# Output projection with four weight operands split once, products in another order over four banks, and the last head's tail in the next block

## The reference, cut to what matters

```python
h = rmsnorm(x, norm1_w); p = h @ w_in                    # x: 2048 x 1024, float32
qa, ka, va, qb, fb, ib, gb = split(p)
ya = window_attention(qa, ka, va)                        # 8 query heads, 2 kv heads, chunks of 64
# group B, 4 heads of 128, chunkwise:
fg = lb + (1 - lb) * sigmoid(fb); kh = 1 - fg; b = cumsum(log(fg)) within a chunk
att = (qh * exp(b - ref)) @ (kh * exp(ref - b)).T, causal
state[n + 1] = exp(b_last) * state[n] + (kh * exp(b_last - b)).T @ vh
yb = rmsnorm(att @ vh + (qh * exp(b)) @ state, g_norm_w) * silu(gb)
x = x + concat(ya, yb) @ w_out
h = rmsnorm(x, norm2_w); x = x + (silu(h @ w_gate) * (h @ w_up)) @ w_down
```

## Time and profile before

| what | value |
|---|---|
| median of three runs | 2230.67 us |
| the profiled execution's own time | 2232.16 us |
| its span, first to last instruction | 2230.4 us |
| PE busy | 2127.2 us (95%), 11512 matmuls |
| DVE busy | 1385.3 us (62%) |
| ACT busy | 908.1 us (41%) |
| mean granted clock of TensorE | 0.981 |
| blocks, and pairs of the projection | 18.1 to 760.6 us, 760.6 to 933 us |
| 1 MB load of an hx, issue to landing | 5.1 us |

### The profile page before, as it was taken

One profiled execution on the slowest core, in us unless ns is written; L12 is line 12 of the kernel. 1 busy time (PEld: TensorE's weight loads), 2 busy tenths in 40 slices (PEclk: granted clock), 3 DMA queues, 4 the chain that ended last, 5 costly groups with the idle time before them and its releaser, 6 DMA issues.

```text
span 2230.4 us, 29485 instructions
## 1 busy us (share of the span) xinstructions
PE 2127.2 (95%) x11512; PEld 1810.7 (81%) x11512; DVE 1385.3 (62%) x2030; ACT 908.1 (41%) x1526; POOL 102.8 (5%) x109
## 2 busy tenths in 40 slices
...
GB/s 264 143 76 57 95 110 67 78 113 76 67 119 90 154 179 244 212 153 131 149 158 151 151 99 168 188 174 170 147 179 137 171 260 179 198 173 187 180 137 90
DMA packets 173979, 327.67 MB, mean 147 GB/s; under 512 B 10321, under 2 KB 105809, under 8 KB 159377
## 3 DMA queue, kind: packets, MB, share of 16 engines
...
## 4 chain that ended last, share of the span: by engine, by line
PE 57%; DMA 0%; issue 0%; DVE 0%; POOLq 0%
PE b_bank_B L328 4%; PE b_bank_A L328 4%; PE b_bank_C L328 4%; PE b_bank_A L329 4%; PE b_bank_C L329 4%; PE b_bank_B L329 4%; PE b_bank_B L330 4%; PE b_bank_A L330 4%; PE b_bank_C L330 4%; PE b_hx_bank L1875 3%; PE b_hx_bank L1874 3%; PE b_hx_bank L1873 3%; PE b_bank_D L328 2%; PE b_bank_D L329 2%; PE b_bank_D L330 2%; PE b_hx_bank L1818 1%
## 5 line engine op out<-in xcount | busy, mean ns | idle before, releaser
L328 PE MATMUL a_pj<-a_w_hi,a_hT_hi 128*128 128x256 f32 x896 | 264.4, 295 | 1.5 <-DVE a_hT_lo L1160 1.5
L329 PE MATMUL a_pj<-a_w_lo,a_hT_hi 128*128 128x256 f32 x896 | 256.9, 287 | 0.0
L330 PE MATMUL a_pj<-a_w_hi,a_hT_lo 128*128 128x256 f32 x896 | 256.9, 287 | 0.0
L1761 ACT ACTIVATE b_s_hi<-b_s_stage 128x1408 fp32r<-128x1408 f32 x56 | 77.4, 1382 | 300.4 <-PE b_hx_bank L1875 150.1
L328 PEld LDWEIGHTS a_pj<-a_w_hi,a_hT_hi 128*128 128x128 f32 x896 | 175.4, 196 | 7.7 <-issue 2.7
L329 PEld LDWEIGHTS a_pj<-a_w_lo,a_hT_hi 128*128 128x128 f32 x896 | 175.5, 196 | 0.0
L330 PEld LDWEIGHTS a_pj<-a_w_hi,a_hT_lo 128*128 128x128 f32 x896 | 175.3, 196 | 0.0
L1146 DVE TENSOR_TENSOR a_w_lo<-a_w_stage,a_w_hi 128x2048 fp32r<-128x2048 f32 (+1 forms) x48 | 101.4, 2112 | 72.1 <-ACT a_w_hi L779 72.1
L328 PE MATMUL b_bank_B<-b_h_hi_T,b_w_hi 128*128 128x512 f32 x352 | 137.3, 390 | 0.0
L328 PE MATMUL b_bank_A<-b_h_hi_B,b_w_hi 128*128 128x512 f32 x352 | 137.3, 390 | 0.0
L330 PE MATMUL b_bank_A<-b_h_hi_B,b_w_lo 128*128 128x512 f32 x352 | 137.0, 389 | 0.0
...
## 6 DMA issues: line engine op xcount, KB each, us to landing
...
```

The lines of the kernel that those rows point to most:

```text
L328: pe.matmul(out, stationary[0](k), moving[0](k), start=(k == 0 and not adds), stop=False, skip_group_check=adds)
L329: pe.matmul(out, stationary[0](k), moving[1](k), start=False, stop=False, skip_group_check=adds)
L330: last = pe.matmul(out, stationary[1](k), moving[0](k), start=False, stop=(k == ends), skip_group_check=adds)
L1761: act.activation(f.s_hi[n % 2][:], f.s_stage[n % 2][:], ACT.Copy).then_inc(f.s_hi_ready, 1)
```

## The change

1. In every block `kt 0` and `ds 0` stand one group earlier. Head 3's `hb` and `hc` stand two groups and one group earlier, ahead of x's scaling; the x transposes 3 to 7 stand behind the last group; head 2's norm and head 3's `ds`, `att`, `o` and norm go behind the next block's first groups.
2. B21, T1, B11 and T2 (the first four operands used) are split once, in blocks 0 to 2: high and low parts are stored to DRAM, and block 3 loads both parts ready-made. Only B22, T4 and T3 are still split in pair 0. The four sets of `w_out` rows are worked on in block 0 (two), block 1 and block 2 (one each) instead of all in block 0.
3. The seven products stand in another order, the bank of each is written down, and a pair has four banks; even pairs use `pj` and `sc`, odd pairs `tr` and `[pvb, hb]`.
4. The squares and the store of a pair's first row come after five of its eight sums.
5. The second `hx` is loaded by SP at the end of the first stage too, and the head of the second stage is ordered anew.

```diff
-    after("G01", 2, ("pt", 4), ("pt", 5), ("sc", 3), ("att", 0), ("sm1", 6), ("sm1", 7), ("hb", 1))
-    after("G01", 3, ("kt", 0), ("sm2", 6), ("sm2", 7), ("pv", 2), ("hc", 1))
-    after("F23", 0, ("ds", 0, 0), ("ds", 0, 1), ("pt", 6), ("pt", 7))
+    after("G01", 2, ("pt", 4), ("pt", 5), ("sc", 3), ("att", 0), ("kt", 0), ("sm1", 6), ("sm1", 7), ("hb", 1))
+    after("G01", 3, ("ds", 0, 0), ("ds", 0, 1), ("sm2", 6), ("sm2", 7), ("pv", 2), ("hc", 1))
+    after("F23", 0, ("pt", 6), ("pt", 7))
...
-    after("I23", 1, ("on2", 1), ("on3", 1), ("split_lo", CHUNK_AT["G23"]), ("kt", 2), ("n1a",))
-    after("I23", 2, ("yt", 1), ("att", 2), ("n1b", 0), ("n1b", 1))
-    after("I23", 3, ("hb", 3), ("n1b", 2), ("n1b", 3))
-    after("G23", 0, ("xT", 0), ("ds", 2, 0), ("ds", 2, 1), ("hc", 3))
-    after("G23", 1, ("xT", 1), ("xT", 2), ("kt", 3))
-    after("G23", 2, ("o", 2), ("on1", 2), ("xT", 3), ("ds", 3, 0), ("ds", 3, 1))
-    after("G23", 3, ("xT", 4), ("xT", 5), ("xT", 6), ("xT", 7), ("on2", 2), ("on3", 2))
+    after("I23", 1, ("on2", 1), ("on3", 1), ("n1a",), ("kt", 2), ("hb", 3), ("split_lo", CHUNK_AT["G23"]))
+    after("I23", 2, ("yt", 1), ("att", 2), ("hc", 3))
+    after("I23", 3, ("n1b", 0), ("n1b", 1), ("n1b", 2), ("n1b", 3))
+    after("G23", 0, ("ds", 2, 0), ("ds", 2, 1))
+    after("G23", 1, ("xT", 0))
+    after("G23", 2, ("o", 2), ("on1", 2), ("kt", 3), ("xT", 1), ("xT", 2))
+    after("G23", 3, ("xT", 3), ("xT", 4), ("xT", 5), ("xT", 6), ("xT", 7))
...
-LAST_HEAD = {("KV", 0): (("att", HG - 1), ("yt", HG - 2)), ("KV", 1): (("o", HG - 1), ("on1", HG - 1)),
-             ("KV", 3): (("on2", HG - 1), ("on3", HG - 1)), ("QA0", 0): (("yt", HG - 1),)}
-PRODUCTS_OUT = ("P1", "P5", "P6", "P3", "P7", "P2", "P4")
+LAST_HEAD = {("KV", 0): (("on2", 2), ("on3", 2), ("ds", 3, 0), ("ds", 3, 1)), ("KV", 1): (("yt", 2), ("att", 3)),
+             ("KV", 2): (("o", 3), ("on1", 3)), ("KV", 3): (("on2", 3), ("on3", 3)), ("QA0", 1): (("yt", 3),)}
+PRODUCTS_OUT = ("P1", "P5", "P2", "P6", "P3", "P4", "P7")
+BANK_OUT = (0, 1, 2, 0, 1, 3, 0)
+READ_OUT = {"P6": 1, "P3": 2, "P7": 4}
+ROW_OUT = (5, 7)
...
+SPLIT_OUT = 4
+WO_BLOCK = (0, 0, 1, 2)
+def out_weight_sums(b):
+    if b == 0:
+        return {("KV", 0): (("wo_load", 0), ("wo_load", 1)), ("KV", 1): (("wo_sums", 0), ("wo_hi", 0)), ("KV", 2): (("wo_lo", 0),),
+                ("KV", 3): (("wo_store", 0), ("wo_sums", 1), ("wo_hi", 1)), ("QA0", 0): (("wo_lo", 1),), ("QA0", 1): (("wo_store", 1),)}
+    k = WO_BLOCK.index(b)
+    return {("KV", 0): (("wo_load", k),), ("KV", 3): (("wo_sums", k), ("wo_hi", k)), ("QA0", 0): (("wo_lo", k),), ("QA0", 1): (("wo_store", k),)}
...
 def out_prepared():
-            ("G23", 3): (("t_load", 4), ("t_load", 5), ("t_load", 6), ("t_hi", 3), ("a_hi", 0, 4), ("a_lo", 0, 2))}
+            ("G23", 3): (("on2", 2), ("on3", 2), ("a_lo", 0, 3), ("ds", 3, 0), ("ds", 3, 1), ("t_load", 4), ("t_load", 5), ("t_load", 6), ("a_hi", 0, 6))}
...
 def out_steps():
-    after(0, 0, ("t_lo", 3), ("a_hi", 0, 5), ("a_hi", 0, 6))
-    after(0, 1, ("t_hi", 4), ("a_load", 1))
-    after(0, 2, ("t_lo", 4), ("t_hi", 5), ("n2w_load",))
-    after(0, 3, ("t_lo", 5), ("t_hi", 6))
-    after(0, 4, ("t_lo", 6))
+    after(0, 0, ("yt", 2), ("att", 3), ("a_lo", 0, 4))
+    after(0, 1, ("o", 3), ("on1", 3), ("t_hi", 4), ("t_lo", 4), ("a_load", 1))
+    after(0, 2, ("t_hi", 5), ("t_lo", 5), ("on2", 3), ("on3", 3), ("a_lo", 0, 5), ("n2w_load",))
+    after(0, 3, ("t_hi", 6), ("t_lo", 6), ("a_lo", 0, 6))
+    after(0, 4, ("yt", 3),)
...
-            after(p, 5, ("a_sum", p + 1, "S4"), ("a_hi", p + 1, 2), ("a_hi", p + 1, 3), ("x_load", p + 1, 0), ("x_load", p + 1, 1), ("a_lo", p + 1, 0))
-            after(p, 6, ("a_hi", p + 1, 4), ("a_lo", p + 1, 1))
+            after(p, 5, ("a_hi", p + 1, 2), ("a_hi", p + 1, 3), ("x_load", p + 1, 0), ("x_load", p + 1, 1), ("a_lo", p + 1, 0), ("a_sum", p + 1, "S4"))
+            after(p, 6, ("a_hi", p + 1, 4), ("a_lo", p + 1, 1), ("a_lo", p + 1, 2))
...
-    out_banks = [pj, sc]
+    out_banks = [pj + sc, tr + [pvb, hb]]
...
+                elif kind == "wo_hi":
+                    k, s = step[1], wo_set(step[1])
+                    act.wait_ge(wo_ready, k + 1)
+                    if k >= 2:
+                        act.wait_ge(o_full.sem, o_full.upto(b - 1, HG))
+                    act.activation(wo_hi[s][:, 0:2, :], wo_blocks[s][:, 2:4, :], ACT.Copy)
+                    act.activation(wo_hi[s][:, 2:4, :], wo_sums[s][:], ACT.Copy).then_inc(wo_hi_ready, 1)
...
                 sp.dma_start(kept.hx[:], hc[0, HC.index(RIGHT[0])]).then_inc(kept.first_hx_loaded, 16)
+                sp.dma_start(kept.second_hx[:], hc[0, HC.index(RIGHT[1])]).then_inc(kept.second_hx_loaded, 16)
...
-        mix_weights(0)
-        w1_low(0)
+        dve.wait_ge(f.gu_loaded[0], 16)
+        w1_low_plain(0)
+        mix_weights(0)
         h_low(0, 0)
+        w1_low_mixed(0)
+        h_low(0, 1)
         w2_low(0)
-        h_low(0, 1)
```

More of the change, by code:

```diff
@@ L152, in of_next_block @@
     return step[0] in ("sq", "n1a", "n1b", "xT") or step[0] in ("split_hi", "split_lo") and step[1] == NW
-def out_weight_sums():
-    return {("KV", 0): (("wo_load", 0), ("wo_load", 1)), ("KV", 1): (("wo_sums", 0),), ("KV", 2): (("wo_store", 0),),
-            ("KV", 3): (("wo_sums", 1),), ("QA0", 0): (("wo_store", 1), ("wo_load", 2)), ("QA0", 2): (("wo_sums", 2), ("wo_load", 3)),
-            ("QA0", 3): (("wo_store", 2),), ("QA1", 0): (("wo_sums", 3),), ("QA1", 1): (("wo_store", 3),)}
-def out_prepared():
-    return {("KV", 0): (("t_load", 0),), ("KV", 2): (("t_hi", 0),), ("QA0", 0): (("t_lo", 0),),
-            ("Q01", 1): (("t_load", 1),), ("F23", 1): (("t_load", 2),), ("Q23", 1): (("t_hi", 1), ("x_load", 0, 0), ("x_load", 0, 1)),
-            ("I23", 0): (("t_lo", 1), ("a_load", 0)), ("I23", 1): (("t_hi", 2),), ("I23", 3): (("t_lo", 2),),
-            ("G23", 0): (("t_load", 3), ("a_sum", 0, "S1"), ("a_sum", 0, "S3")),
-            ("G23", 1): (("a_hi", 0, 0), ("a_hi", 0, 1), ("a_sum", 0, "S2"), ("a_sum", 0, "S4")),
-            ("G23", 2): (("a_hi", 0, 2), ("a_hi", 0, 3), ("a_lo", 0, 0), ("a_lo", 0, 1)),
-            ("G23", 3): (("t_load", 4), ("t_load", 5), ("t_load", 6), ("t_hi", 3), ("a_hi", 0, 4), ("a_lo", 0, 2))}
@@ new lines, in out_prepared @@
+def out_prepared():
+    return {("KV", 0): (("t_load", 0),), ("Q01", 1): (("t_load", 1),), ("F23", 1): (("t_load", 2),),
+            ("Q23", 1): (("x_load", 0, 0), ("x_load", 0, 1), ("a_load", 0)),
+            ("I23", 3): (("a_sum", 0, "S1"), ("a_sum", 0, "S3")),
+            ("G23", 0): (("t_load", 3), ("a_sum", 0, "S2"), ("a_sum", 0, "S4"), ("a_hi", 0, 0), ("a_hi", 0, 1)),
+            ("G23", 1): (("a_lo", 0, 0), ("a_hi", 0, 2), ("a_hi", 0, 3)),
+            ("G23", 2): (("a_lo", 0, 1), ("a_lo", 0, 2), ("a_hi", 0, 4), ("a_hi", 0, 5)),
+            ("G23", 3): (("on2", 2), ("on3", 2), ("a_lo", 0, 3), ("ds", 3, 0), ("ds", 3, 1), ("t_load", 4), ("t_load", 5), ("t_load", 6), ("a_hi", 0, 6))}
@@ L210, in out_steps @@
             after(p + 2, 1, ("mix", p, 3), ("mix_store", p))
-        after(p, 6, ("mid", p))
+        after(p, 5, ("mid", p, 0))
+        after(p, 6, ("mid", p, 1))
     after(OUT_PAIRS - 1, 0, ("next_loads",))
@@ L435, in build_phase_a @@
     wo_sums = [put(f"a_wo_sums{s}", [P, 2, 512], F32, at=at) for s, at in enumerate((spare_lo, f_at + 8192))]
+    wo_hi = [put(f"a_wo_hi{s}", [P, SPLIT_OUT, 512], F32R, at=at) for s, at in enumerate((i_at + 8192, i_at))]
     half = KT // 2 * TB * 4
@@ L454, in build_phase_a @@
     n2w = put("o_n2w", [P, D], F32, at=y_at)
+    kept.second_hx = put("b_hx1", [P, 4, 512], F32, at=y_at)
+    kept.second_hx_at = y_at
     mix_t = put("o_mix_t", [P, 3, 512], F32, at=y_at + D * 4)
```

205 lines of the change are left out of this document (116 added, 89 removed).

## The result

The kernel after takes 2159.56 us, median of 4 runs (2158.44 to 2159.83), beside 2231.24 us for the kernel before in the same comparison (2227.15 to 2232.1): a ratio of 0.9681, 95% interval 0.9665 to 0.9698, so 3.2% or about 71.7 us less. Forecast were 2154 us and a range of 2140 to 2180. One of the four executions of the run with part 1 undone took 3023.82 us at a granted clock of 0.654, in a slow state; it is left out of that run's median.

A forecast was written before the change was run, and what follows sets the result against it. The prediction took the kernel to be bound by PE's own program, busy 2127.2 of 2230.4 us. Terms 38.4 + 27.6 + 1.6 - 1.0 + 7.1 + 1.0 + 5.1 = 79.8, less 2.8, gave gain 77: 2154 us, range 2140 to 2180.

The forecast's parts named there:

- part 1: att 0 to pv 3, every block: kt 0 and ds 0 one group earlier; 9.6 us a block, 38.4 in all.
- late next: What PE waits for after the change; behind the state chain the softmax, pt 6 0.9 us and pt 7 0.6.
- Rival (a): Softmax and copies replace the chain as PE's wait, so less is gained in blocks: 2182 us, chance 0.17.
- Part 2: Blocks 0 to 2, from att 2: head 3's gates earlier, its ds, att, o in the next block; 27.6 us.
- 37.3 - 26.6 - 1.2 = 9.5: Block 1, att 2 to att 3: length less PE's work less small stands; 9.2 us taken as gain.
- Part 3: Weight operands split in blocks 0 to 2: front gains 1.6 us, blocks 1 and 2 lose 1.0.
- rival (d): F0's copy in blocks 1 and 2 waits for its stores, 10 us a block: 2174 us, chance 0.03.
- Part 4: Block 3's end and pair 0: no gates wait, three operands split; pair 1 begins 7.1 us earlier.
- Part 5: Pairs: product order, four banks, split mid; DVE's sum stays near 20.9 us, gain 1 us in all.
- rival (c): Pauses between products in four banks keep PE at 1.2 GHz in the pairs: 2252 to 2311 us, chance 0.02.
- Part 6: Hand-over to the second stage: second hx load's wait goes, DVE is late next; first product 5.1 us sooner.
- The charge for the lower clock: Deduction of 2.8 us because remaining stands in each F23 and pair 0 can bring the lower clock.

The follow-up runs named there:

- part 1 undone: Kernel after with kt 0 and ds 0 back at their old places in all four blocks: 2199.64 us, ratio 0.9863.
- the two experiments: kt 0 and ds 0 put back in the kernel after (40.1 us above it), and moved alone in the kernel before (39.4 us less than it).
- part 1 alone: Kernel before with only kt 0 and ds 0 one group earlier: 2192.06 us, ratio 0.9829.
- the run with late splits: Kernel after with all seven weight operands loaded raw and split in block 3 and pair 0, sums made in block 0 alone: 2158.75 us, ratio 0.968.
- the two-bank run: Kernel after with two banks for each pair's products, their order kept, output not the reference's: 2159.44 us, ratio 0.9683.
- the order run: Kernel after with the second stage's head reordered, hx 0's low part ahead of the plain low part and two mixing operations: 2156.96 us, ratio 0.9674.

## Why the prediction was right, and where its terms were off

**What bounds it, and part 1: right in mechanism and size.** 38.4 forecast, 38.8 read from the trace, 39.4 and 40.1 by the two experiments. The hand-followed order held to 0.1 us for the chain, and the stands that were named as "late next" are the ones seen: kt 0 1.03 us (1.1 forecast), pt 6 0.58 (0.9), pt 7 0.44 (0.6). Rival (a), the softmax in the chain's place, would have needed stands of 5 us; with the softmax put first, the cost was 2.9 us in all.

**Part 2: right in mechanism, too large by some 3 us.** 22.8 us plus the 1.8 us that the weight sets take in two of these stretches are 24.6, against 27.6. The step "37.3 - 26.6 - 1.2 = 9.5" held as far as it went: it puts KV's second group 27.8 us behind att 2, and 28.3 was measured. What failed is the list of small stands: it ends there and puts the next one at nothing. Head 2's `yt` was taken as work that follows freely; it waits for the end of head 3's state chain, which reads the state products of ds 3 on DVE, and ds 3 had just been moved to the group before. Moving `yt` behind att 3 gave 0.9 us a block, 2.7 of the 3.0 missing.

**Part 3: the loss in blocks 1 and 2 larger, the front's gain not shown.** Blocks 1 and 2 lost 1.8 us (0.9 each) instead of 1.0. The copy's delay was read correctly (0.5 forecast, 0.66 seen); the remaining 0.25 us of each 0.9 is not accounted for by a stand. The front won 0.9 us instead of 1.6. In stands it lost 0.3: 2.85 and 0.21 us for low parts of weights went, 1.40 and 1.96 came. What it won is the lower clock behind the 2.85 us, and that differs from one execution to the next (0.91 in the kernel before, 1.00 behind 2.77 us with part 1 alone). The last store was issued at 47.1 us and not near 41, and F0's copy still doesn't wait for it: in block 0 it waits for PE. ACT waits for no store there in blocks 1 and 2 either, so rival (d) is out. As forecast, part 3 is worth little: the run with late splits came out the same.

**Part 4: right in mechanism, too large by 2.2 us.** 4.9 instead of 7.1. The stands that it names came near (for P4's 2.2 us there is one of 1.38 us, for head 3's norm, at `yt` 3 ahead of it; 0.90 for 1.0; 1.64 for 1.9), but `yt` 2's stand of 1.51 us is the same omission as in part 2. Its repair gave 0.9 us. The other 1.3 us are not in G23: 3.7 us from att 2 to the end of I23, 15.3 for G23 and 1.1 for ds 3 are 20.1, and the trace has 692.07 - 671.82 = 20.25. They lie in pair 0: the forecast left 55.3 - 7.1 - 20.1 = 28.1 us for it, and it took 30.13. Its stands were 5.4 us together and the forecast's 5.1, so some 1.7 us are outside any stand, in PE's own steps of pair 0, which the count priced too low. Which of them is open.

**Part 5: 2.4 instead of 1.0**, and not by the banks, which the two-bank run shows to be worth nothing. The traces show pairs 1 to 4 at 19.8, 20.3, 20.5 and 20.5 us where they were 20.6, 21.0, 21.4 and 21.0; pair 5 is 20.4 where it was 19.8. The ready-made operands didn't do it either, since the run with late splits has the same pairs. The stands did change: before, PE stood 0.53, 1.28, 1.56 and 1.27 us ahead of pairs 2 to 5 for `a_lo 0`, the low part of a pair's first operand. Now it stands 0.54, 0.62, 0.68 and 0.63 us ahead of their second product. One of each, before and after:

```profile
853.07 0.50 PE L328 MATMUL a_pj<-o_t_hi,o_a_hi 128*128 128x512 f32 x1 [1.56 <-DVE o_a_lo L1344]
```

```profile
786.47 0.50 PE L342 MATMUL a_pj<-o_t_hi,o_a_hi 128*128 128x512 f32 x1 [0.68 <-DVE o_a_lo L1387]
```

The 2.2 us between the two sums are nearly the 2.4 of the gain. That fits the step which the prediction names, `a_lo 0` put ahead of a sum, but no run parts it from the order of products and the split `mid`. So the freed banks, the first reason that the prediction gives, brought nothing, and its bound of 20.9 us a pair by DVE's operations did not hold: pairs 1 to 4 took 19.8 to 20.5. The clock was 1.00 in every stretch of 20 us from 720 to 860 us with four banks and with two, so rival (c) is out. The rule of the Trainium skill's page "TensorE: Matmul & The Clock Gate", section "A second HAM failure mode: psum-queue depth-cycling", does not show here: PE stood 0.5 to 0.7 us once in each of pairs 2 to 5, and its clock was 1.00 in all of them.

**Part 6: 3.5 instead of 5.1.** "What is late next is DVE" is right: the first product waits for the low part of hx 0, behind five operations, and the order run had 2.3 us less of that stand. What the term lacked is PE's speed: the second turn took 3.47 us and not 2.1. It came behind 3.03 and 3.39 us of standing with 1.94 us of work between them, in the stretch with a clock of 0.91.

**The charge for the lower clock** of 2.8 us was too high for this execution: the clock was 1.00 everywhere but at the hand-over, where it cost about 1.5 us (3.47 less 1.94). With the same stands in the front it fell there too in two of eight executions, for 0.6 to 1.5 us. This error hid part of the errors above: the terms were 6.1 us too large together, the charge made it 3.3. That the total came so near is in this part luck. By the medians, the gain is 71.7 us and the forecast time of 2154 is 5.6 us too low.
